# Attention units taken by TensorE two at a time instead of one at a time

## The chip, the cores and the metric

The kernel runs on one core of a Trainium2 chip. A core has TensorE (matrix products), VectorE, ScalarE and GpSimd (elementwise work), and queues that issue transfers. The engines run side by side, each through its own instruction list in order, and they meet only at semaphores: counters that one engine raises and another waits for. The profile calls the engines PE (TensorE; PEld are its weight loads), DVE (VectorE), ACT (ScalarE) and POOL (GpSimd). The metric is the device time of one execution in microseconds.

## What is computed

Two transformer blocks of two layers each, for 512 tokens of width 1024. Four of their parts are softmax attention, and only they bear on the change. The reference, cut to them:

```python
def dsa_mixer(...):                      # 12 heads, keys picked by an indexer
    s = jnp.einsum('bthd,btkd->bthk', qi, k_sel) * HEAD_DIM ** -0.5
    p = masked_softmax(s, valid[:, :, None, :]).astype(v.dtype)
    return jnp.einsum('bthk,btkd->bthd', p, v_sel)
def memory_attention(q_mem, mem_n, w_kv_mem):   # 4 heads, 256 keys, in both layers of the first block
    s = jnp.einsum('bshd,bnhd->bhsn', q, k).astype(jnp.float32) * HEAD_DIM ** -0.5
    p = jax.nn.softmax(s, axis=-1).astype(v.dtype)
    return jnp.einsum('bhsn,bnhd->bshd', p, v)
def nsa_mixer(...):                      # 12 heads, three branches, gated sum
    o = gi[..., 0:1] * o_c + gi[..., 1:2] * o_s + gi[..., 2:3] * o_w
def swa_sink_mixer(...):                 # 16 heads, this and the preceding 128 keys, a sink
    p = e / (jnp.sum(e, axis=-1, keepdims=True) + jnp.exp(sink - mx))
    o = jnp.einsum('bnkgqs,bnskd->bnqkgd', p.astype(vb.dtype), vb)
```

Everything else (projections, feed-forward parts, gated linear attention, norms) is the same before and after.

## The kernel before

**Stages.** The program is one long sequence. Most of it is 368 tiles of weights that stream in and are multiplied on TensorE (line 764). In between stand three stages of attention: stage one (names `dsa` and `mem0`), stage two (`nsa0`, `nsa1`, `mem1`) and stage three (`swa0`, `swa1`). `STREAMS` lists them and `UNITS` gives the number of units: 48, 16, 54, 54, 16, 32 and 32, in all 252.

**A unit** is one block of 128 queries of one head (in `nsa` also one of its branches) against its key tiles of 128 keys. In `dsa` the four units of a head have 1, 2, 3 and 4 key tiles. In `nsa` a head has nine units: a compressed one (one tile), and then 3, 3, 4, 4, 1, 1, 2 and 2 tiles. In `mem` every unit has 2, in `swa` a head's four units have 1, 2, 2 and 2.

**Steps of a unit g.** It passes through six steps on three engines:

- *scores* on PE (lines 955, 967): queries times keys into a score bank. There are four such banks (three for `nsa`).
- *maximum* on DVE (lines 2139, 2175): masks and finds the row maximum, written to `nmax`.
- *exponentials* on ACT (line 1583; 1579 for the compressed unit): writes the exponentials into one of two buffers, `prob[g % 2]` (the trace calls it `tmp`), and then reads out the row sum, which is the record ACTIVATION_READ_ACCUMULATOR. It waits for the maximum and for the transposes of unit g-2, which read the same buffer.
- *transposes* on PE (line 979): one per key tile, into `probT_bank[g % 2]`. They wait for the exponentials of g and for the move of g-2, which empties that bank.
- *move* on ACT (line 1598; in `dsa` and `mem` every fourth one is on DVE, line 2186): from that bank into the buffer `probT[g % 2]` (the trace calls it `sq`). It waits for the transposes of g and for the values of g-2, which read that buffer.
- *values* on PE (lines 1008, 995): transposed exponentials times values. They wait for the move of g. After them comes the output on DVE (lines 2269, 2265, 2246), which normalises.

In the trace a values product of one key tile is two MATMUL records.

**Order.** `attention_stream` (line 201) runs the same loop on each engine, with a body written for each. With u the step, ahead 4 (5 in `swa`, function `look_ahead`), the bodies are:

- PE: scores of u+4, transposes of u+2, values of u
- ACT: exponentials of u+3, move of u+2
- DVE: maximum of u+4, now and then a move of u+2, output of u

GpSimd stages the queries of the next pair of heads (lines 644 to 652) and otherwise waits in these stages. No weights are split and no product of line 764 runs in them.

Of the kernel before, what the change touches and what calls it, by code (L numbers as in the profile page):

```python
# [165 lines left out]
def attention_unit(kind, u):  # L166

    if kind.startswith("nsa"):
        hh, r = divmod(u, 9)  # L170
        return (hh, NSA_ORDER[(r - 1) // 2], 1 + (r - 1) % 2) if r else (hh, 0, 0)
    return u // 4, u % 4, 1

def compressed(kind, u):
    return kind.startswith("nsa") and u % 9 == 0
# [7 lines left out]
def look_ahead(kind):  # L184

    return 5 if kind.startswith("swa") else 4
# [7 lines left out]
def bank_of(kind, u):  # L194

    if compressed(kind, u):
        return 3
    return u % (3 if kind.startswith("nsa") else 4)
# [31 lines left out]
def key_tiles(kind, qt, branch):  # L230

    if kind.startswith("mem"):
        return list(range(N_MEM // P))
    if kind.startswith("swa"):
        return [qt - 1, qt] if qt else [0]
    return list(range(qt + 1))

def program(nc, A):
    with ExitStack() as ctx:  # L240
# [171 lines left out]
        def output_place(kind, u, g):  # L412

            if kind.startswith("swa"):
                return o_bank[g // TT % 2][:, HD * (u % TT):HD * (u % TT + 1)]
            return o_bank[g % 2][:, 0:HD]
# [144 lines left out]
        def staged(kind):  # L562

            return {"d": q_stage0, "n": q_stage1, "s": q_stage2}[kind[0]]
# [184 lines left out]
        def _(pe):  # L749
# [178 lines left out]
            def scores(kind, pair, u, i):  # L928
                hh, qt, br = attention_unit(kind, u)
                per, o, l = PER_PAIR[kind], HD * hh, int(kind[3]) if kind[3:] else 0  # L930
                g = UNIT0[kind] + pair * per + u
                out = score_bank[bank_of(kind, u)]
                if u % (per // 2) == 0:

                    pe.wait_ge(q_staged, STAGED[kind] + 2 * pair + hh + 1 + 2 * i)

                if g or not isinstance(i, int):
                    pe.wait_ge(probs_ready, g - kind.startswith(("dsa", "mem0", "swa")) + per * i)
                if compressed(kind, u):  # L940

                    if hh:
                        return
                    of_blocks = masks_b[:, 2 * P:3 * P].rearrange("p (a c) -> p a c", a=TT).unsqueeze(2).to_broadcast([P, TT, 2, 32])
                    nc.tensor.matmul(out[:, 0:2 * P], ident_b[:, :], of_blocks, start=True, stop=False)
                    for a in range(TT):
                        r = nc.tensor.matmul(out[:, 64 * a:64 * a + 64], q_pos0[:, a * P:(a + 1) * P], k_cmp[:, l, :], start=False, stop=a == TT - 1)
                    r.then_inc(scores_ready, 1)
                    return
                kts = key_tiles(kind, qt, br)  # L950
                n = len(kts) * P
                if kind.startswith("mem"):
                    if u == 0:
                        pe.wait_ge(mem_scaled, l + 1)
                    nc.tensor.matmul(out[:, 0:n], q_plain[o:o + HD, qt * P:(qt + 1) * P], k_mem[o:o + HD, l, pair, :],
                                     start=True, stop=True).then_inc(scores_ready, 1)
                    return

                q = staged(kind)[:, hh, qt * P:(qt + 1) * P]
                if kind == "dsa":  # L960
                    ks = [k[:, 0:n] for k in k_dsa]
                elif kind.startswith("swa"):
                    ks = [k[:, l, kts[0] * P:(qt + 1) * P] for k in k_swa]
                else:
                    ks = [k[:, 2 * (br - 1) + l, 0:n] for k in k_nsa]
                for part, k in enumerate(ks):
                    r = nc.tensor.matmul(out[:, 0:n], q, k, start=part == 0, stop=part == 1)  # L967

                r.then_inc(scores_ready, 2 if kind.startswith("nsa") and u == 10 else 1)

            def transposes(kind, pair, u, i):
                _, qt, br = attention_unit(kind, u)
                per = PER_PAIR[kind]
                g = UNIT0[kind] + pair * per + u
                pe.wait_ge(probs_ready, g + 3 + per * i)

                pe.wait_ge(probT_ready[g % 2], g // 2 + 1 + per // 2 * i)
                for n in range(1 if compressed(kind, u) else len(key_tiles(kind, qt, br))):
                    r = nc.tensor.transpose(probT_bank[g % 2][:, n * P:(n + 1) * P], prob[:, g % 2, n * P:(n + 1) * P], ident[:, :])  # L979
                r.then_inc(transposed, 1)  # L980

            def values(kind, pair, u, i):
                hh, qt, br = attention_unit(kind, u)
                per, l = PER_PAIR[kind], int(kind[3]) if kind[3:] else 0
                g = UNIT0[kind] + pair * per + u
                pe.wait_ge(probT_ready[g % 2], g // 2 + 2 + per // 2 * i)
                if not kind.startswith("swa"):

                    pe.wait_ge(o_done, g + 1 + per * i)
                elif u % TT == 0:  # L990

                    pe.wait_ge(o_done, g - 2 + per * i)
                if compressed(kind, u):

                    r = nc.tensor.matmul(o_bank[g % 2][:, 0:TT * HD + TT], probT[:, g % 2, 0:P], v_cmp[:, l, :], start=True, stop=True)
                    r.then_inc(pv_done, 1)
                    return
                kts = key_tiles(kind, qt, br)
                for n, kt in enumerate(kts):
                    if kind == "dsa":  # L1000
                        v = dsa_v[:, kt, :]
                    elif kind.startswith("mem"):
                        v = v_mem[:, l, kt, (2 * pair + hh) * HD:(2 * pair + hh + 1) * HD]
                    elif kind.startswith("swa"):
                        v = sv[:, kt, l * HD:(l + 1) * HD]
                    else:
                        v = v_nsa[:, kt, (br - 1) * P + l * HD:(br - 1) * P + (l + 1) * HD]
                    r = nc.tensor.matmul(output_place(kind, u, g), probT[:, g % 2, n * P:(n + 1) * P], v, start=n == 0, stop=n == len(kts) - 1)  # L1008
                r.then_inc(pv_done, 1)
# [13 lines left out]

            def pair_of_heads(per, at):

                for u in range(per):
                    later = u + look_ahead(at(u)[0])
                    if at(later):
                        scores(*at(later))
                    if at(u + 2):  # L1030
                        transposes(*at(u + 2))
                    values(*at(u))

            def concat(n, prefix, kind, units, follow, hs):

# [187 lines left out]
            def banks_free():  # L1223
                wait_evacuated(pe, "qmem0.1")

            attention_stream(pe, STREAMS[0], lambda at: attention_begin(at, banks_free), pair_of_heads)
            for l in range(DEPTH):
                if l == 1:
# [51 lines left out]
                    def banks_free():  # L1280
                        for name in ("gatesT", "qmem1.1"):
                            wait_evacuated(pe, name)

                    attention_stream(pe, STREAMS[1], lambda at: attention_begin(at, banks_free), pair_of_heads)
                concat(l, f"cat{l}", f"mem{l}", UNIT0[f"mem{l}"] + 16, f"wo{l}.0", (cat_hi, cat_lo))
                for j in range(1, KT):
# [1596 lines left out]
```

## Time and profile before

| what | value |
|---|---|
| time, median of 3 runs | 2467.14 us (2463.45 to 2471.73) |
| span of the profiled execution | 2468.0 us |
| PE busy | 2423.7 us (98%) |
| DVE busy | 936.0 us (38%) |
| ACT busy | 1079.6 us (44%) |
| POOL busy | 972.3 us (39%) |
| stage one of attention, from the trace | 144.54 to 226.22 us |
| stage two | 743.43 to 894.70 us |
| stage three | 1979.25 to 2039.27 us |

The profile is one execution; its span is 0.9 us above the median of the runs. Busy shares over the whole span mix stages with different limits, so the argument is made inside the three stages. A row of the timeline is one instruction or a run of like instructions: start, duration, engine, line, operation, output<-inputs, shapes, count, and in brackets the idle time before it with what ended that. Records of PE are pipelined: the time from the start of one to the start of the next is what it costs, and its duration, which includes the way through the array, is what somebody who waits for the result sees.

### The profile page before, as it was taken

How to read it: one execution, taken by the hardware profiler on the slowest of the kernel's cores; microseconds unless marked ns; L12 is line 12 of the kernel's file. 1: busy time of each engine (PE TensorE's matmuls, PEld its weight loads, DVE VectorE, ACT ScalarE, POOL GpSimd, SP SyncE).
4: the chain of work that ended last, by engine and by line, in shares of the span. 5: the costliest groups of instructions: out<-in, count | busy, mean ns of one | idle time of the engine just before them, and what ended most of it. 6: DMA issues, size and time to landing. Idle time of an engine off the chain costs nothing.

```text
span 2468.0 us, 36248 instructions
## 1 busy us (share of the span) xinstructions
PE 2423.7 (98%) x11990; PEld 2004.0 (81%) x11990; DVE 936.0 (38%) x2051; ACT 1079.6 (44%) x1917; POOL 972.3 (39%) x484
## 2 busy tenths in 40 slices
PE   8999999999999999999999999999999999999998
PEld 6888888888778978888887978788888797788886
DVE  7976322211477753222214243321211773311212
ACT  7565443432347754444335534432332583432321
POOL 4821444444331124444443413444443423444441
PEclk9999999999999999999999999999999999999999
DMA  4300333333420013233332312233333202233331
GB/s 154 116 30 18 90 97 101 94 102 105 128 69 10 1 35 94 93 102 93 103 102 79 103 39 81 77 95 95 100 94 94 69 18 69 86 101 95 94 94 68
DMA packets 57866, 202.75 MB, mean 82 GB/s; under 512 B 7072, under 2 KB 7968, under 8 KB 57392
## 3 DMA queue, kind: packets, MB, share of 16 engines
q1 hardware_dynamic: 54864, 196.02, 26.2%
q10 hardware_dynamic: 2912, 5.55, 0.6%
q8 instruction: 55, 0.90, 0.1%
q14 instruction: 35, 0.29, 0.0%
HBM read 199.44 MB, written 2.10 MB: 82 GB/s over the span
## 4 chain that ended last, share of the span: by engine, by line
PE 41%; issue 14%; POOL 7%; ACT 1%; DVE 1%; POOLq 0%; DVEq 0%; ACTq 0%
PE bank L764 36%; POOL w_lo L618 7%; PE bank L1008 1%; PE bank L967 1%; PE bank L979 1%; ACT h_hi L1492 1%; PE bank L1372 0%; PE bank L1353 0%; ACT gained L1495 0%; PE bank L1367 0%; PE bank L793 0%; PE bank L1055 0%; PE bank L881 0%; PE bank L770 0%; PE bank L786 0%
## 5 line engine op out<-in xcount | busy, mean ns | idle before, releaser
L618 POOL TENSOR_TENSOR w_lo<-w_raw,w_hi 128x1024 fp32r<-128x1024 f32 x368 | 883.3, 2401 | 1197.7 <-ACT w_hi L1449 1188.1
L764 PE MATMUL bank<-h_hi,w_hi 128*128 128x512 f32 x1648 | 650.5, 395 | 7.2 <-DVE tmp L2476 2.1
L764 PE MATMUL bank<-h_lo,w_hi 128*128 128x512 f32 x1648 | 642.2, 390 | 0.0
L764 PE MATMUL bank<-h_hi,w_lo 128*128 128x512 f32 x1648 | 642.2, 390 | 0.0
L1449 ACT ACTIVATE w_hi<-w_raw 128x1024 fp32r<-128x1024 f32 x368 | 386.8, 1051 | 242.7 <-PE bank L764 214.0
L764 PEld LDWEIGHTS bank<-h_hi,w_hi 128*128 128x128 f32 x1648 | 309.8, 188 | 82.3 <-issue 5.9
L764 PEld LDWEIGHTS bank<-h_hi,w_lo 128*128 128x128 f32 x1648 | 309.7, 188 | 65.2
L764 PEld LDWEIGHTS bank<-h_lo,w_hi 128*128 128x128 f32 x1648 | 309.9, 188 | 65.0 <-issue 2.2
L764 PE MATMUL bank<-mact_hi,w_hi 128*128 128x512 f32 x512 | 199.3, 389 | 1.7 <-DVEq L2342 1.7
L764 PE MATMUL bank<-mact_hi,w_lo 128*128 128x512 f32 x512 | 199.2, 389 | 0.0
L764 PE MATMUL bank<-mact_lo,w_hi 128*128 128x512 f32 x512 | 199.2, 389 | 0.0
L764 PE MATMUL bank<-act_hi,w_hi 128*128 128x512 f32 x352 | 136.9, 389 | 0.0
L764 PE MATMUL bank<-act_lo,w_hi 128*128 128x512 f32 x352 | 136.9, 389 | 0.0
L764 PE MATMUL bank<-act_hi,w_lo 128*128 128x512 f32 x352 | 136.9, 389 | 0.0
L1583 ACT ACTIVATE tmp<-bank,nmax 128x128 f32<-128x128 f32 (+2 forms) x240 | 119.1, 496 | 19.7 <-DVE nmax L2139 12.0
L2340 DVE TENSOR_TENSOR tmp<-sq,bank 128x512 f32<-128x512 f32 x64 | 44.0, 688 | 200.2 <-ACT sq L1661 200.2
L1647 ACT ACTIVATE act_hi<-tmp 128x512 f32 x44 | 27.8, 632 | 207.6 <-DVE tmp L2327 207.6
L764 PEld LDWEIGHTS bank<-mact_hi,w_hi 128*128 128x128 f32 x512 | 96.1, 188 | 21.8 <-issue 1.8
L1598 ACT ACTIVATE sq<-bank 128x128 f32<-128x128 f32 (+3 forms) x232 | 92.7, 401 | 48.1 <-PE bank L1008 44.8
L764 PEld LDWEIGHTS bank<-mact_lo,w_hi 128*128 128x128 f32 x512 | 96.1, 188 | 19.9
L764 PEld LDWEIGHTS bank<-mact_hi,w_lo 128*128 128x128 f32 x512 | 96.1, 188 | 19.8
L979 PE MATMUL bank<-ident,tmp 128*128 128x128 f32 x548 | 107.1, 284 | 3.6 <-ACT tmp L1583 1.5
(403 smaller groups left out, 3489.3 us busy)
## 6 DMA issues: line engine op xcount, KB each, us to landing
w_raw<-in_weights SPq DMA_DIRECT2D x368, 512.0 KB, 3.6
out<-x ACTq DMA_DIRECT2D x8, 256.0 KB, 2.1
x<-in_xT SPq DMA_DIRECT2D x4, 256.0 KB, 6.8
x<-in_xT ACTq DMA_DIRECT2D x4, 256.0 KB, 7.4
memx<-in_memT SPq DMA_DIRECT2D x1, 1024.0 KB, 9.8
cmp_w1k<-in_cmp_w ACTq DMA_DIRECT2D x1, 1024.0 KB, 5.6
cmp_w1v<-in_cmp_w ACTq DMA_DIRECT2D x1, 1024.0 KB, 7.5
rope_c<-in_rope_c SPq DMA_DIRECT2D x1, 256.0 KB, 8.4
```

The source lines that it names most:

```text
L618: nc.gpsimd.tensor_tensor(w_lo[:, t % RING, :], w_raw[:, t % RAW, :], w_hi[:, t % RING, :].bitcast(F32), ALU.subtract).then_inc(lo_ready, 1)
L764: r = nc.tensor.matmul(out, a, b, start=first and n == 0, stop=last and n == 2)
L967: r = nc.tensor.matmul(out[:, 0:n], q, k, start=part == 0, stop=part == 1)
L979: r = nc.tensor.transpose(probT_bank[g % 2][:, n * P:(n + 1) * P], prob[:, g % 2, n * P:(n + 1) * P], ident[:, :])
L1008: r = nc.tensor.matmul(output_place(kind, u, g), probT[:, g % 2, n * P:(n + 1) * P], v, start=n == 0, stop=n == len(kts) - 1)
L1449: nc.scalar.activation(w_hi[:, t % RING, :], w_raw[:, t % RAW, :], ACT.Copy).then_inc(hi_ready, 1)
L1492: nc.scalar.activation(h_hi[:, k, :], x_bank(k) if k < BY_PE else x[:, k, :], ACT.Identity, scale=col(name, k)).then_inc(gain_rounded, 1)
L1583: nc.scalar.activation(prob[:, g % 2, 0:n], score_bank[bank_of(kind, u)][:, 0:n], ACT.Exp, bias=nmax[:, s4:s4 + 1], scale=1.0 if kind.star ...
L1598: nc.scalar.activation(probT[:, g % 2, 0:n], probT_bank[g % 2][:, 0:n], ACT.Copy).then_inc(probT_ready[g % 2], 1)
L1647: nc.scalar.activation(act_hi[:, bass.ds(2 * i + f, 1), :].rearrange("p a n -> p (a n)"), tmp[:, f, :], ACT.Copy).then_inc(act_rounded, 1)
L2340: nc.vector.tensor_tensor(tmp[:, f % 2, :], sq[:, f % 2, :], bank[b % 2][:, :], ALU.mult).then_inc(act_made, 1)
```

## The change

Only the loop body of TensorE is written anew. It takes two steps at once: the scores of both, then the transposes of both, then the values of both. No instruction is added or removed, and the bodies of the other engines, the buffers and all the semaphore counts stay as they are.

```diff
             def pair_of_heads(per, at):
 
-                for u in range(per):
-                    later = u + look_ahead(at(u)[0])
-                    if at(later):
-                        scores(*at(later))
-                    if at(u + 2):
-                        transposes(*at(u + 2))
-                    values(*at(u))
+                for u in range(0, per, 2):
+                    for n in (u, u + 1):
+                        later = n + look_ahead(at(n)[0])
+                        if at(later):
+                            scores(*at(later))
+                    for n in (u, u + 1):
+                        if at(n + 2):
+                            transposes(*at(n + 2))
+                    for n in (u, u + 1):
+                        values(*at(n))
```

In stage one, on PE, two steps of `dsa` stood before as follows (scores are the rows with k_dsa, transposes those with ident, values those with dsa_v):

```order
L967 MATMUL bank<-k_dsa_hi,q_stage 128x128
L967 MATMUL bank<-k_dsa_lo,q_stage 128x128
L979 MATMUL bank<-ident,tmp 128x128 x3
L1008 MATMUL bank<-dsa_v,sq 128x64
L967 MATMUL bank<-k_dsa_hi,q_stage 128x256
L967 MATMUL bank<-k_dsa_lo,q_stage 128x256
L979 MATMUL bank<-ident,tmp 128x128 x4
L1008 MATMUL bank<-dsa_v,sq 128x64 x2
```

The same two steps now, in the same engine's list:

```order
L967 MATMUL bank<-k_dsa_hi,q_stage 128x128
L967 MATMUL bank<-k_dsa_lo,q_stage 128x128
L967 MATMUL bank<-k_dsa_hi,q_stage 128x256
L967 MATMUL bank<-k_dsa_lo,q_stage 128x256
L979 MATMUL bank<-ident,tmp 128x128 x7
L1008 MATMUL bank<-dsa_v,sq 128x64 x3
```

The one value product that stood between the transposes of three and of four tiles has moved behind all seven of them, and the second scores have moved ahead of the first transposes.

In stage two, on PE, where a head of `nsa` begins (v_cmp is the values product of the compressed unit), before:

```order
L967 MATMUL bank<-k_nsa_hi,q_stage 128x512
L967 MATMUL bank<-k_nsa_lo,q_stage 128x512
L979 MATMUL bank<-ident,tmp 128x128 x3
L995 MATMUL bank<-v_cmp,sq 128x260
L967 MATMUL bank<-k_nsa_hi,q_stage 128x128
L967 MATMUL bank<-k_nsa_lo,q_stage 128x128
L979 MATMUL bank<-ident,tmp 128x128 x4
L1008 MATMUL bank<-v_nsa,sq 128x64 x3
```

And now:

```order
L967 MATMUL bank<-k_nsa_hi,q_stage 128x512
L967 MATMUL bank<-k_nsa_lo,q_stage 128x512
L967 MATMUL bank<-k_nsa_hi,q_stage 128x128
L967 MATMUL bank<-k_nsa_lo,q_stage 128x128
L979 MATMUL bank<-ident,tmp 128x128 x7
L995 MATMUL bank<-v_cmp,sq 128x260
L1008 MATMUL bank<-v_nsa,sq 128x64 x3
```

Here too the values of the first unit (v_cmp) now stand behind the transposes of the unit after next but one, with its four tiles.

## Rows read from the trace of the kernel before

**Rows 1.** The page, busy time, share of the span and instructions of each engine

```profile
PE 2423.7 (98%) x11990; PEld 2004.0 (81%) x11990; DVE 936.0 (38%) x2051; ACT 1079.6 (44%) x1917; POOL 972.3 (39%) x484
```

**Rows 2.** Windows (stretch, length; busy PE, PEld, DVE, ACT, POOL; clock, DMA): dsa, mem0, nsa, swa

```profile
146.97:199.84 52.87, 52.29 (x419) 48.64 (x418) 42.08 (x187) 40.37 (x125) 7.72 (x12) 1.00 0.00 0
...
206.17:221.43 15.26, 15.26 (x90) 10.88 (x89) 9.62 (x37) 8.01 (x30) 1.47 (x2) 1.00 0.00 1
...
747.11:869.60 122.49, 121.54 (x971) 112.24 (x968) 97.30 (x432) 95.11 (x304) 14.54 (x17) 1.00 0.00 1
...
1992.31:2031.52 39.21, 39.21 (x351) 39.04 (x350) 31.87 (x146) 37.33 (x157) 9.63 (x24) 1.00 0.00 1
```

**Rows 3.** The timeline of all engines in dsa

```profile
163.09 0.56 PE L1008 MATMUL bank<-dsa_v,sq 128*128 128x64 f32 x4
...
163.74 0.60 ACT L1598 ACTIVATE sq<-bank 128x512 f32<-128x512 f32 x1 [0.21 <-PE bank L1008]
...
163.89 0.27 PE L979 MATMUL bank<-ident,tmp 128*128 128x128 f32 x1
164.00 0.78 PE L1008 MATMUL bank<-dsa_v,sq 128*128 128x64 f32 x6
...
164.24 0.47 ACT L1583 ACTIVATE tmp<-bank,nmax 128x256 f32<-128x256 f32 x1
...
164.59 0.48 PE L967 MATMUL bank<-k_dsa_hi,q_stage 128*128 128x512 f32 x1
...
164.90 0.39 PE L967 MATMUL bank<-k_dsa_lo,q_stage 128*128 128x512 f32 x1
...
165.13 0.38 PE L979 MATMUL bank<-ident,tmp 128*128 128x128 f32 x2
165.18 0.28 DVE L2269 TENSOR_SCALAR o_tok<-bank,rinv 128x64 f32 x1 [0.15 <-DVE rinv L2252]
165.35 1.00 PE L1008 MATMUL bank<-dsa_v,sq 128*128 128x64 f32 x8
165.48 0.70 DVE L2139 CUSTOM_DVE_ANT_0 bank<-bank,dsa_mask 128x512 f32<-128x512 f32 x1
...
166.09 0.14 DVE L2139 DVE_READ_ACCUMULATOR2_ANT nmax<- 128x1 f32 x1
...
166.27 0.69 ACT L1583 ACTIVATE tmp<-bank,nmax 128x512 f32<-128x512 f32 x1 [0.55 <-DVE nmax L2139]
...
168.45 0.20 ACT L1583 ACTIVATION_READ_ACCUMULATOR tmp<-bank,nmax 128x1 f32 x1
...
168.77 0.33 PE L979 MATMUL bank<-ident,tmp 128*128 128x128 f32 x1
...
168.93 0.82 PE L1008 MATMUL bank<-dsa_v,sq 128*128 128x64 f32 x6
```

**Rows 4.** Groups by shape on ACT in dsa: count, busy, mean ns, idle before

```profile
L1583 ACT ACTIVATE tmp<-bank,nmax 128x512 f32<-128x512 f32 x12 | 8.2, 687 | 5.8 <-DVE nmax L2139 5.8
...
L1598 ACT ACTIVATE sq<-bank 128x512 f32<-128x512 f32 x11 | 6.5, 594 | 1.3 <-PE bank L1008 1.1
...
L1583 ACT ACTIVATE tmp<-bank,nmax 128x128 f32<-128x128 f32 x11 | 4.0, 367 | 2.8 <-DVE nmax L2139 2.2
L1598 ACT ACTIVATE sq<-bank 128x128 f32<-128x128 f32 x12 | 3.3, 276 | 1.4 <-PE bank L1008 0.9
```

**Rows 5.** The timeline of PE in nsa, the values of a compressed unit

```profile
863.98 0.60 PE L995 MATMUL bank<-v_cmp,sq 128*128 128x260 f32 x2
```

**Rows 6.** The timeline of PE where stage one begins, scores in a row

```profile
145.49 0.40 PE L967 MATMUL bank<-k_dsa_hi,q_stage 128*128 128x512 f32 x1
145.72 0.40 PE L967 MATMUL bank<-k_dsa_lo,q_stage 128*128 128x512 f32 x1
```

**Rows 7.** Windows where stage three begins, columns as in rows 2

```profile
1979.25:1984.48 5.23, 3.59 (x24) 2.64 (x23) 4.16 (x17) 3.46 (x13) 2.61 (x3) 1.00 0.32 100
1984.48:1991.49 7.01, 7.01 (x37) 7.01 (x36) 4.79 (x16) 5.35 (x19) 0.90 (x3) 0.51 0.00 1
```

## The prediction, made before the changed kernel was run

> **What bounds the kernel now.** I read the page first: PE is busy for 98% of the span [rows 1]. The change touches only the attention stages, so the second view is the table of windows for their steady parts. In `dsa` (44 steps) PE is busy 52.29 of 52.87 us, ACT 40.37 and DVE 42.08; in `nsa` (104 steps) 121.54 of 122.49, against 95.11 and 97.30; in `mem0` (11 steps) 15.26 of 15.26 against 8.01; in `swa` (48 steps) 39.21 of 39.21, against 37.33 on ACT [rows 2]. A step thus takes 1.20, 1.18, 1.39 and 0.82 us. PE sets it everywhere, but only in `mem` with much room: the other two engines work for about four fifths of each step, and in `swa` ACT for 95%. The third view, the timeline, shows how they fit. ACT starts a move 0.09 us after the values product that frees its buffer has ended (163.09 + 0.56 = 163.65, the move at 163.74), and PE starts transposes 0.12 us after the exponentials' sum is read (168.65, then 168.77) [rows 3]. Those hand-overs lie beside other work now, because each engine has one whole step of slack against the other.
>
> **What the change adds and removes.** It removes no instruction. On PE alone it can save the switches between kinds of work. A pair of score products of four tiles costs 0.31 + 0.23 us behind a values product (164.59, 164.90, 165.13) [rows 3], and 0.23 for the first of the two when scores stand in a row (145.49, 145.72) [rows 6]. That is 0.08 us a pair of units, and one switch each from transposes to values and from values to scores goes too, for which I allow 0.05 together. So PE alone would save about 0.13 x 126 pairs = 16 us.
>
> **What it does to the order.** Call a the first unit of a pair. PE now does scores a+4, a+5; transposes a+2, a+3; values a, a+1. ACT still does move a+2, exponentials a+4, move a+3, exponentials a+5, move a+4. Follow the buffers. Move a+2 needs the values of a (same `probT`). The transposes of a+5 need the exponentials of a+5. The values of a+2 now stand behind the transposes of a+5 on PE, where they stood behind those of a+4. And move a+4, the very next item on ACT after exponentials a+5, needs the values of a+2. This is a closed ring, once per two units:
>
> values a end, 0.09, move a+2, exponentials a+4, move a+3, exponentials a+5, 0.12, transposes a+5, values a+2 end.
>
> Before, the ring went through the transposes of a+4, so move a+3 and exponentials a+5 ran on ACT while PE did transposes and values. Now all of ACT's work for two units and the round trip through PE stand one behind the other. Queued behind the waiting transposes on PE are the values of two units; behind the waiting move on ACT is everything ACT has; and the outputs on DVE follow the values.
>
> **Prices of the links.** Exponentials of one tile take 0.37 us, of four 0.69, so 0.47 and 0.58 between; a move takes 0.28 to 0.59 [rows 4]. What follows a move starts 0.10 us before its recorded end (163.74 to 164.24 for 0.60), and the read-out of a sum adds 0.10 to exponentials that somebody waits for [rows 3]. Transposes cost 0.11 us a tile (163.89 to 164.00; 165.13 to 165.35) and 0.05 more after a wait (168.77 to 168.93 for one). Values take 0.56, 0.78 and 1.00 us for two, three and four tiles, so 0.34 for one [rows 3], and 0.60 for the compressed unit [rows 5].
>
> **dsa.** With a the unit of one tile: 0.09 + move of three tiles 0.39 + exponentials of one 0.37 + move of four 0.50 + exponentials of two 0.47 + 0.10 + 0.12 + transposes of two 0.27 + values of three 0.78 = 3.09 us. With a the unit of three tiles, DVE is later than ACT, since its maximum of a+5 stands behind the output of a, and the move of a+3 is its own: 0.09 + output 0.30 + maximum of four tiles 0.75 + 0.04 (165.18, 165.48, 166.23, 166.27 [rows 3]) + exponentials 0.79 + 0.12 + transposes of four 0.49 + values of one 0.34 = 2.92. A head takes 6.01 instead of 4.81 us, and 44 steps are 11 heads: **+13 us**. From below, if the round trip hides 0.2 us of each ring, +9; from above, if one hand-over more of 0.2 us falls into each, +18.
>
> **nsa.** Two heads are 18 units and nine rings. The moves sum to 5.8 us (16 of them at 0.18 to 0.50, two compressed at 0.18), the exponentials to 8.4 and, as an estimate for the two compressed ones, 0.4, the nine read-outs to 0.9 and the nine double hand-overs to 1.9. The transposes of a+5 have 21 tiles in the nine rings, so 2.3 + 9 x 0.05 = 2.8, and the values of a+2 sum to 0.78 + 1.00 + 0.34 + 0.56 + 0.78 + 1.00 + 0.34 + 0.56 + 0.60 = 6.0. That is 26.2. In three or four rings DVE's maximum, or the eight products of the compressed scores on PE, comes later than ACT; I add 0.4 and take 26.6 against 18 x 1.18 = 21.2. With 104 steps, 5.8 such groups: **+31 us**, with +26 and +37 as ends.
>
> **swa.** PE is five ahead here and ACT four, so exponentials a+6 fill the round trip, and the ring is 0.09 + move a+2 + exponentials a+5 + move a+3 + 0.12 + transposes a+5 + values a+2: 0.09 + 0.27 + 0.47 + 0.37 + 0.12 + 0.27 + 0.56 = 2.15 us, and with a move and values of one tile 1.83, to which the exponential of the sink adds some 0.1. A head takes 4.07 instead of 3.27 us. With 59 steps that is +11.8, less a little for the five that stand at the lower clock already: **+11 us**, with +7 and +15 as ends.
>
> **mem.** PE takes 2.78 us for two units. The ring is 0.09 + 0.28 + 0.47 + 0.28 + 0.47 + 0.10 + 0.12 + 0.27 + 0.56 = 2.64, so PE still sets the time: **0**, with -3 (the switches) and +3 as ends.
>
> The PE-only saving is not added anywhere, since PE waits in each of these rings; if `mem` shows it, it is in the -3. GpSimd's staging and the weights' queue gain time and stay hidden: POOL is busy 7.72 of 52.87 us and waits for scores [rows 2].
>
> **Sum.** 13 + 31 + 11 + 0 = 55 us. The profiled execution would go from 2468.0 to 2523, and the median of the runs, 0.9 us lower, from 2467 to 2522. The ends of the terms together give +39 to +73.
>
> **Rivals.**
>
> *The clock falls (slower still).* Where stage three begins, PE was busy 3.59 of 5.23 us and then ran 7.01 us at a granted clock of 0.51, which is mostly the lower level of 1.2 GHz against 2.4; that stretch holds five steps, 1.40 us each against 0.82 [rows 7], [rows 2]. After the change PE will be without work for about a fifth of three stages, some 300 us. For it: PE busy shares there come near those 69%. Against it: the idle is in slices of half a microsecond between runs of products, and the present stages hold the full clock. A step at the low clock costs 1.40 us where I expect 1.0 in `swa`. If a fifth of about 280 us ran so, +20 us more, so 2542; if half did, +50, so 2572. The Trainium skill, "TensorE: Matmul & The Clock Gate", section "A second HAM failure mode: psum-queue depth-cycling", says that frequent short idles between groups of matmuls make the clock swing between its levels; by that rule this rival is the likelier one. The granted clock of 1.00 through the four stretches of rows 2 neither shows nor excludes it, since PE is never short of work there.
>
> *PE's own saving decides (faster).* If ACT and DVE kept up, the switches would be all that counts: 2467 - 16 = 2451. It decides where the ring of two units is shorter than PE's work for two: below 2.4 us in `dsa`, where I find 2.9 to 3.1. For it: ACT has a fifth of its time free in `dsa` and `nsa`, and the buffers are not fewer. Against it: the ring is made of waits that the code fixes, and ACT's free fifth is no help to it, since the ring puts that time where ACT has nothing it may start. The Trainium skill, same page, section "Loop structure matters more than you think", recommends dense runs of PE work with the other engines behind; by it the answer would be this rival's.
>
> *The slack swallows it (no change).* If half a step of slack were left that I do not see, each ring would fall back under PE's time, and saving and waits would cancel: 2467, at most 7 to either side.
>
> *A milder loss.* If in `nsa` the moves, short for units of one tile, let ACT run ahead, so that only every second ring closes: 13/2 + 31/2 + 11/2 = 28, so 2495.
>
> **Chances.** My ring 0.74, the clock 0.13, the milder loss 0.07, no change 0.02, PE's saving 0.04. About 0.3%, or 7 us, is what a measurement of this kernel can tell from no change. So faster 0.04, same 0.02, slower 0.94. The range takes the ends of the sum, +39 to +73, is widened below to +33 for part of the milder case, and reaches above to +93 for the clock in a fourth of the stages: 2500 to 2560.
>
> **What would show it.** In the profile of the changed kernel, windows in `dsa`, `nsa` and `swa` should show PE busy near 80% and ACT near what it had in microseconds, with step times of 1.50, 1.48 and 1.02 us, and `mem` unchanged near 1.39. The waits should show transposes of odd units waiting for exponentials, and ACT's moves of even units waiting for values for 0.8 to 1.5 us each. The ring is wrong if PE stays over 95% busy there, if the moves wait for something else, or if the added time lies outside the stages. A granted clock below 1 in the steady parts would show the first rival.

## The result, and the profile after

The changed kernel takes 2519.65 us (median; 2518.39 to 2523.78), against 2468.76 us for the kernel before in the same comparison. The ratio is 1.0212, with a 95% interval of 1.0198 to 1.0226. The profiled execution went from a span of 2468.0 us to 2518.0.

The page of the changed kernel has as first line, busy time, share and instructions, where [rows 1] stood:

```profile
PE 2441.4 (97%) x11990; PEld 2001.7 (79%) x11990; DVE 930.1 (37%) x2051; ACT 1070.8 (43%) x1917; POOL 972.2 (39%) x484
```

That line hides the change. PE's busy time is even larger by 18 us. A record of PE reaches past the start of the next one (transposes of one tile last 0.27 us where the next start is 0.11 on, [rows 3]), and ahead of a wait nothing covers that tail: in `dsa` 22 waits go with 3.3 us more busy time. The instructions of ACT and DVE are the same in number, and their busy times within 1%. The time shows in windows. These are the five stretches of attention in the changed kernel, in the columns of [rows 2]: `dsa` from its first step, `mem0` to the end of its stage, `nsa`, `mem1`, and the whole of `swa`:

```profile
148.74:213.34 64.60, 55.63 (x421) 48.54 (x419) 40.14 (x186) 37.65 (x124) 8.12 (x12) 1.00 0.00 0
213.34:238.56 25.22, 23.95 (x156) 19.24 (x155) 15.15 (x67) 13.44 (x50) 2.52 (x2) 1.00 0.01 2
758.05:912.18 154.13, 136.99 (x970) 114.05 (x968) 96.37 (x432) 90.49 (x304) 14.97 (x17) 1.00 0.00 1
912.18:937.22 25.04, 23.66 (x145) 17.52 (x144) 14.26 (x63) 13.00 (x50) 2.52 (x2) 1.00 0.01 1
2021.69:2090.51 68.82, 59.59 (x468) 52.47 (x466) 45.46 (x198) 52.88 (x211) 13.66 (x31) 1.00 0.03 9
```

The first and the third answer to the lines of `dsa` and `nsa` in [rows 2]. For the other three, the kernel before has, from scores of the same units to the same place:

```profile
199.84:226.22 26.38, 25.78 (x156) 18.90 (x155) 16.02 (x65) 14.17 (x48) 2.88 (x3) 1.00 0.01 2
...
869.60:894.75 25.15, 24.55 (x145) 17.67 (x144) 15.92 (x61) 13.83 (x49) 2.99 (x3) 1.00 0.00 1
1979.25:2039.27 60.02, 57.18 (x468) 55.57 (x466) 45.97 (x198) 52.31 (x211) 13.54 (x31) 0.94 0.03 10
```

So `dsa` went from 52.87 to 64.60 us (+11.7), `mem0` by -1.2, `nsa` from 122.49 to 154.13 (+31.6), `mem1` by -0.1 and `swa` from 60.02 to 68.82 (+8.8). That sums to 50.8 us where the spans differ by 50.0: the whole loss lies inside the attention stages. PE's weight loads (the second of the busy figures) fall from 92% of the stretch to 75% in `dsa` and to 74% in `nsa`, and ACT from 76% and 78% to 58% and 59%. Nobody is busier; everybody waits.

For whom is in the waits of the changed kernel (its lines from 1030 on are three higher than before: 1601 is the move, 1586 the exponentials, 2142 the maximum, 2272 the output). Columns: who waited for whom, us in total, times, longest. First `dsa`, 22 pairs:

```profile
ACT sq L1601 <- PE bank L1008: 23.7, 22, 1.2
DVE o_tok L2272 <- PE bank L1008: 19.0, 22, 1.4
PEld bank L979 <- ACT tmp L1586: 14.4, 22, 0.8
```

Then `nsa`, 52 pairs:

```profile
ACT sq L1601 <- PE bank L1008: 55.9, 51, 1.4
...
PEld bank L967 <- ACT tmp L1586: 19.7, 36, 0.8
...
PEld bank L979 <- ACT tmp L1586: 13.7, 30, 0.7
...
ACT sq L1601 <- PE bank L995: 7.2, 6, 1.2
```

Once in each pair ACT's move waits 1.1 us for values, and in `dsa` once in each pair PE waits for exponentials before transposes. Each waits for the other in turn. In `nsa` PE stands more often before scores (line 967, 36 times) than before transposes (30 times). By the code, with three score banks the second scores of the next pair, a+7, need the bank that exponentials a+4 read, and these follow the move that waits for the values of a. It is the same ring, met one item earlier on PE: at 800.03 us scores have waited 0.64 us for exponentials, and at 801.08 the transposes behind them wait 0.15 more.

The ring's two turns of one head, from the timeline of the changed kernel in `dsa`:

```profile
174.30 0.49 ACT L1601 ACTIVATE sq<-bank 128x384 f32<-128x384 f32 x1 [0.92 <-PE bank L1008]
...
174.68 0.36 ACT L1586 ACTIVATE tmp<-bank,nmax 128x128 f32<-128x128 f32 x1
...
175.03 0.60 ACT L1601 ACTIVATE sq<-bank 128x512 f32<-128x512 f32 x1
...
175.50 0.48 ACT L1586 ACTIVATE tmp<-bank,nmax 128x256 f32<-128x256 f32 x1
...
175.86 0.22 ACT L1586 ACTIVATION_READ_ACCUMULATOR tmp<-bank,nmax 128x1 f32 x1
176.13 0.44 PE L979 MATMUL bank<-ident,tmp 128*128 128x128 f32 x2 [0.45 <-ACT tmp L1586]
...
176.41 1.67 PE L1008 MATMUL bank<-dsa_v,sq 128*128 128x64 f32 x14
177.28 0.28 ACT L1601 ACTIVATE sq<-bank 128x128 f32<-128x128 f32 x1 [1.20 <-PE bank L1008]
...
177.65 0.70 DVE L2142 CUSTOM_DVE_ANT_0 bank<-bank,dsa_mask 128x512 f32<-128x512 f32 x1
...
178.44 0.69 ACT L1586 ACTIVATE tmp<-bank,nmax 128x512 f32<-128x512 f32 x1 [0.32 <-DVE nmax L2142]
...
179.28 0.66 PE L979 MATMUL bank<-ident,tmp 128*128 128x128 f32 x4 [0.35 <-ACT tmp L1586]
...
179.77 0.78 PE L1008 MATMUL bank<-dsa_v,sq 128*128 128x64 f32 x6
180.20 0.49 ACT L1601 ACTIVATE sq<-bank 128x384 f32<-128x384 f32 x1 [0.98 <-PE bank L1008]
```

Read it from the top: move, exponentials, move, exponentials on ACT without a gap; 0.05 us after the sum is read, PE's transposes; then the values (the record of 14 holds those of two units, three and four tiles); and 1.20 us after ACT had stopped, the next move. From move to move the first turn takes 2.98 us and the second, in which ACT also waits 0.32 us for DVE's maximum, 2.92.

### The profile page after: what moved, and what is told of

Read it like the earlier page. It is cut to its first block, busy times and chain, and to the rows that moved or that the text cites. A ratio compares the mean times of both kernels' runs of the same rounds, so it can differ in the third digit from the quotient of the medians.

```text
span 2518.0 us, 36242 instructions
## 1 busy us (share of the span) xinstructions
PE 2441.4 (97%) x11990; PEld 2001.7 (79%) x11990; DVE 930.1 (37%) x2051; ACT 1070.8 (43%) x1917; POOL 972.2 (39%) x484
## 4 chain that ended last, share of the span: by engine, by line
PE 39%; issue 15%; POOL 7%; ACT 2%; DVE 1%; POOLq 0%; ACTq 0%; DVEq 0%
PE bank L764 35%; POOL w_lo L618 6%; PE bank L1008 1%; PE bank L979 1%; PE bank L1375 0%; ACT h_hi L1495 0%; ACT tmp L1586 0%; ACT sq L1601 0%; PE bank L1356 0%; PE bank L1370 0%; PE bank L793 0%; ACT gained L1498 0%; PE bank L798 0%; PE bank L881 0%; PE bank L770 0%
## 5 line engine op out<-in xcount | busy, mean ns | idle before, releaser
L979 PE MATMUL bank<-ident,tmp 128*128 128x128 f32 x548 | 101.6, 284 | 25.5 <-ACT tmp L1586 16.8
```

## The experiments

All are made on the order of one part at a time, or on one tie at a time. The table gives, from the trace of each, the time from the first scores of a kind to the first scores of the next kind, or to the end of the stage (first turning of the outputs), and the median time with its ratio to the kernel before, run beside it. In `swa` the kernel before had a stretch at the low clock [rows 7] that no other profile in the table has; the others are to be held against the 57.3 us of scores_paired and not against its 60.0.

| kernel | dsa | mem0 | nsa | mem1 | swa | time, us | ratio (95% interval) |
|---|---|---|---|---|---|---|---|
| before | 55.3 | 26.4 | 125.3 | 25.2 | 60.0 | 2466 to 2469 | |
| the changed kernel | 67.0 | 25.2 | 156.9 | 25.0 | 68.8 | 2519.65 | 1.0212 (1.0198 to 1.0226) |
| scores_paired | 55.2 | 23.8 | 131.1 | 22.9 | 57.3 | 2467.25 | 1.000 (0.9991 to 1.001) |
| transposes_paired | 69.8 | 28.1 | 161.2 | 26.9 | 69.0 | 2530.56 | 1.0259 (1.0242 to 1.0276) |
| after_four | 63.7 | 24.5 | 148.0 | 23.5 | 62.9 | 2499.51 | 1.0134 (1.0117 to 1.0151) |
| after_ahead | 57.4 | 25.9 | 157.0 | 25.2 | 68.8 | 2512.97 | 1.0187 (1.0170 to 1.0204) |
| after_five | 57.4 | 25.9 | 145.8 | 27.0 | 68.5 | 2499.95 | 1.0135 (1.0118 to 1.0152) |
| after_four_five | 55.1 | 25.2 | 135.6 | 25.8 | 62.7 | 2481.88 | 1.0063 (1.0046 to 1.0080) |
| after_all | 53.1 | 24.9 | 125.2 | 24.3 | 59.3 | 2463.60 | 0.9991 (0.9982 to 1.0001) |
| before_five | 52.9 | 27.4 | 122.1 | 26.1 | 57.3 | 2462.08 | 0.9978 (0.9968 to 0.9987) |
| before_four_five | 52.6 | 27.2 | 120.7 | 25.9 | 57.0 | 2459.88 | 0.9972 (0.9962 to 0.9981) |
| mix_two | 51.2 | 24.5 | 122.1 | 24.8 | 57.0 | 2455.83 | 0.9951 (0.9936 to 0.9966) |
| best_mix | 50.6 | 24.3 | 120.7 | 24.6 | 56.7 | 2452.96 | 0.9946 (0.9933 to 0.9960) |

**Scores alone in pairs** (scores_paired), the edit against the kernel before:

```diff
-                for u in range(per):
-                    later = u + look_ahead(at(u)[0])
-                    if at(later):
-                        scores(*at(later))
-                    if at(u + 2):
-                        transposes(*at(u + 2))
-                    values(*at(u))
+                for u in range(0, per, 2):
+                    for n in (u, u + 1):
+                        later = n + look_ahead(at(n)[0])
+                        if at(later):
+                            scores(*at(later))
+                    for n in (u, u + 1):
+                        if at(n + 2):
+                            transposes(*at(n + 2))
+                        values(*at(n))
```

> Only the scores are taken two at a time: scores a+4, a+5, then transposes a+2, values a, transposes a+3, values a+1. The ring theory: values of a+2 again stand right behind the transposes of a+4, so no ring closes; what is left is the switch saved, about 0.08 us a pair in 100 pairs, so some 8 us under the kernel before: 2460 (2455 to 2468), and at least 50 us under the changed kernel. The rival, that having two scores in a row holds up the others (banks, a later start of the transposes): half or more of the 51 us loss stays, over 2490.

Measured: 2467.25 us, inside the range but at its upper end, and the same as before. The loss is not in the pairs of scores. But the 8 us of saved switches are not there either. In `swa`, where PE has no idle time, one pair reads:

```profile
2012.69 0.36 PE L967 MATMUL bank<-k_swa_hi,q_stage 128*128 128x256 f32 x1
2012.89 0.28 PE L967 MATMUL bank<-k_swa_lo,q_stage 128*128 128x256 f32 x1
2013.01 0.28 PE L967 MATMUL bank<-k_swa_hi,q_stage 128*128 128x256 f32 x1
2013.13 0.28 PE L967 MATMUL bank<-k_swa_lo,q_stage 128*128 128x256 f32 x1
2013.25 0.38 PE L979 MATMUL bank<-ident,tmp 128*128 128x128 f32 x2
2013.47 0.33 PE L1008 MATMUL bank<-sv,sq 128*128 128x64 f32 x2
2013.66 0.41 PE L979 MATMUL bank<-ident,tmp 128*128 128x128 f32 x2
2013.91 0.56 PE L1008 MATMUL bank<-sv,sq 128*128 128x64 f32 x4
2014.27 0.36 PE L967 MATMUL bank<-k_swa_hi,q_stage 128*128 128x256 f32 x1
```

The second product of the second scores starts 0.12 us after the first, where it takes 0.20 behind values: that is the 0.08 I had counted. But now transposes stand behind values, and there the same price is paid: a one-tile values product takes 0.19 us to the next start and a two-tile run of transposes 0.25, against 0.14 and 0.22 in the other order. PE still leaves values twice a pair, once for scores and once for transposes, and the pair takes 1.58 us (2012.69 to 2014.27) where the same pair takes 1.59 in the order one at a time; the last section has both. In `nsa` the stretch is even 5.8 us longer. It has three score banks, and scores wait there for exponentials; the waits of that stretch have

```profile
PEld bank L967 <- ACT tmp L1585: 9.6, 23, 0.5
```

where the kernel before has no such wait among its largest. That these waits are the 5.8 us was not tested by itself; ACT's moves wait longer there too. In the two `mem` stretches pairs of scores do save, 2.6 and 2.3 us.

**Transposes alone in pairs** (transposes_paired), the edit against the changed kernel:

```diff
-                    for n in (u, u + 1):
-                        later = n + look_ahead(at(n)[0])
-                        if at(later):
-                            scores(*at(later))
+                    if at(u + look_ahead(at(u)[0])):
+                        scores(*at(u + look_ahead(at(u)[0])))
                     for n in (u, u + 1):
                         if at(n + 2):
                             transposes(*at(n + 2))
-                    for n in (u, u + 1):
-                        values(*at(n))
+                    values(*at(u))
+                    if at(u + 1 + look_ahead(at(u + 1)[0])):
+                        scores(*at(u + 1 + look_ahead(at(u + 1)[0])))
+                    values(*at(u + 1))
```

> Only the transposes are taken two at a time: scores a+4, transposes a+2, a+3, values a, scores a+5, values a+1. The ring theory: values of a+2 stand behind the transposes of a+5 as in the changed kernel, so the whole loss is there without pairs of scores or values: 2520 (2510 to 2532). The rival, that the loss comes from scores or values in pairs: under 2490.

Measured: 2530.56 us, in the range, and 11 us over the changed kernel. So the loss needs neither pairs of scores nor adjacent values; two runs of transposes ahead of the values are enough. That it is worse still fits the second scores standing between the values of a and those of a+1, for which move a+3 waits; it was not tested by itself.

**More buffers between move and values** (after_four). The transposed exponentials get four buffers (three in `nsa` and `mem1`), in space of the activations that is unused during attention:

```diff
+            k = u % 3 if kind.startswith("nsa") else (u + 3) % 4 if kind == "mem1" else g % 4
+            return sq[:, k, part] if k < 2 else more_T[:, k - 2, part]
...
-                act.wait_ge(pv_done, g + 1 + per * i)
-                nc.scalar.activation(probT[:, g % 2, 0:n], probT_bank[g % 2][:, 0:n], ACT.Copy).then_inc(probT_ready[g % 2], 1)
+                moves_free(act, kind, g, per, i)
+                nc.scalar.activation(probT_of(kind, u, g, slice(0, n)), probT_bank[g % 2][:, 0:n], ACT.Copy).then_inc(probT_ready[g % 2], 1)
```

`moves_free` waits for the values of four (three) units back.

> The changed kernel with four buffers for the transposed exponentials (three in nsa and mem1), so that a move waits for the values of four (three) units back and not of two. Ring theory: the link from values to the next move is gone. In swa nothing else ties the engines, so its whole loss goes (about -10 us). In dsa and nsa a second ring stays, through DVE: values a, output a, maximum a+5, exponentials a+5, transposes a+5, values a+2: 0.09 + 0.30 + 0.6 + 0.04 + 0.65 + 0.12 + 0.33 + 0.67 = 2.8 us a pair, against 2.9 to 3.0 now and 2.4 before; so -5 us in dsa and -5 to -10 in nsa. In all 2498 (2488 to 2508). If the buffers had nothing to do with it: 2520 with no stage changed. If they were the only tie: about 2460.

Measured: 2499.51 us, 20 us off the changed kernel's time with PE's order untouched. `dsa` gave back 3.3 us where I had put 5, and `nsa` 8.9. The second ring, through DVE, is in the waits of `dsa` in this kernel (line 1600 is the exponentials, 2286 the output, 1022 the values):

```profile
ACT tmp L1600 <- DVE nmax L2156: 18.8, 29, 1.2
DVE o_tok L2286 <- PE bank L1022: 15.7, 22, 1.2
```

ACT no longer waits 23.7 us for values. It waits for maxima, and once in each pair DVE's output, which stands before the maximum, waits for values. `swa` gave back 5.9 us, not all: something else ties it too. The timeline of `swa` in this kernel shows it (the transposes are line 993):

```profile
2030.67 0.37 ACT L1600 ACTIVATE tmp<-bank,nmax 128x128 f32<-128x128 f32 x1 [0.65 <-PE bank L993]
...
2034.38 0.37 ACT L1600 ACTIVATE tmp<-bank,nmax 128x128 f32<-128x128 f32 x1 [0.66 <-PE bank L993]
```

Exponentials wait for the transposes of two units back, which read the same one of two buffers.

**Five ahead** (after_ahead in `dsa` and `mem0`, after_five everywhere):

```diff
-    return 5 if kind.startswith("swa") else 4
+    return 5 if kind.startswith("swa") or kind in ("dsa", "mem0") else 4
```

> The changed kernel with dsa and mem0 five scores ahead as swa is (exponentials four ahead), buffers as they were. Ring theory: exponentials a+6 now fill the round trip, and DVE's maximum a+5 comes before output a. Rings of a dsa head: 0.09 + 0.39 + 0.47 + 0.60 + 0.12 + 0.27 + 0.78 = 2.72 and about 2.4 (PE's own), so 5.1 us a head instead of 5.9: -9 us, in dsa alone: 2511 (2507 to 2515). The rival, that PE's own order costs the time: 2520 unchanged.

Measured: 2512.97 us; `dsa` went from 67.0 to 57.4 us (-9.6), `mem0` grew by 0.7. That is a test inside one kernel: `nsa` and `swa`, which were not edited, stayed at 157.0 and 68.8.

> The changed kernel with five scores ahead in every kind, so in nsa and mem1 too (which have three score banks); buffers as they were. Ring theory: in nsa exponentials a+6 fill the round trip and the ring is 0.09 + 0.33 + 0.53 + 0.43 + 0.12 + 0.31 + 0.66 = 2.5 us a pair on average against 3.0 in the changed kernel: -25 us in nsa beside the -9 in dsa: 2488 (2480 to 2500). The rival, that nsa is held by its three banks of scores: no gain over five ahead in dsa alone, 2513.

Measured: 2499.95 us, at the upper end. `nsa` gave back 11 us, not 25. So five ahead is not enough there.

**Both together** (after_four_five).

> The changed kernel with both: four (three) buffers and five ahead everywhere. Ring theory: the ring over ACT and the one over DVE are both open, so PE's own work sets the time again with the order two at a time in full: no more than before, 2455 to 2470. If taking two units at a time costs PE itself something: 2480 or more remains.

Measured: 2481.88 us, 12 us over the range. Here my theory of two rings fell short: `dsa` was at the kernel before's time (55.1 us), but `nsa` was 10 us and `swa` some 5 over what PE needs. The next run asks whether that is the tie that after_four had shown, or PE's order itself.

**More buffers for the exponentials too** (after_all), against after_four_five:

```diff
-                act.wait_ge(transposed, g + 1 + per * i)
+                deep = 3 if kind.startswith("nsa") or kind == "mem1" else 4
+                free = g + 3 - deep
+                act.wait_ge(transposed, max(free, 1) if isinstance(i, int) and not i else free + per * i)
```

> The changed kernel, five ahead everywhere, four (three) buffers for the transposed exponentials and now also four (three) for the exponentials themselves, so that exponentials wait for the transposes of four (three) units back. What is left of the loss with five ahead and the first four buffers is 13 us, +10 in nsa and +5 in swa. If it is the tie from transposes to the exponentials of two units on (a third ring): swa falls to the kernel before's and nsa by half or more, in all 2470 (2464 to 2475). If it is the score banks, or PE's order in itself: 2479 to 2484 as before this edit.

Measured: 2463.60 us, ratio 0.9991, just below the range. With the changed order of PE in full, and only waits taken out of the other engines' way by buffers and by looking ahead, the kernel is as fast as the kernel before. `nsa` is at 125.2 us with three score banks as ever, so the banks alone did not hold it. Windows of `dsa`, `nsa` and `swa` in this kernel:

```profile
145.92:198.98 53.06, 51.98 (x415) 48.67 (x413) 40.52 (x188) 39.56 (x125) 7.39 (x11) 1.00 0.00 0
739.52:864.68 125.16, 123.76 (x964) 114.39 (x963) 92.59 (x433) 94.01 (x305) 13.72 (x16) 1.00 0.02 5
1971.84:2031.18 59.34, 56.02 (x468) 52.44 (x466) 44.70 (x198) 51.47 (x211) 14.01 (x31) 1.00 0.04 10
```

PE is at 98%, 99% and 94% of them, and its weight loads, the better measure of the two, at 92%, 91% and 88%.

**The same edits in the order one at a time** (before_five, before_four_five).

> The kernel before with five ahead everywhere. PE waits for transposes there for some 10 to 15 us in dsa and nsa, most of it behind late maxima; those go: 2459 (2454 to 2467). If PE's idle there is its own: 2467.

> The kernel before with five ahead everywhere and four (three) buffers for the transposed exponentials. No ring is near PE's time there, so the buffers add nothing to five ahead: within 3 us of it, 2459. If the buffers matter in the order one at a time too: 2450 or less.

Measured: 2462.08 and 2459.88 us. Five ahead is worth 0.2%, in `dsa` (-2.4 us) and `nsa` (-3.1); the buffers, worth 20 us in the changed kernel, give about 2 here, with overlapping intervals. These two are also the fair measure of after_all, which has the same look-ahead and one more set of buffers: at 0.9991 (0.9982 to 1.0001) it does not reach the 0.9972 (0.9962 to 0.9981) of before_four_five. The two intervals only just miss each other. In the traces `nsa` is at 125.2 us against 120.7 and `swa` at 59.3 against 57.0, and the `mem` stretches give back 3.9 of these 7 us. So even with the slack bought, taking all of the work two at a time is no faster than one at a time. What still costs it time in `nsa` and `swa` is left open.

**A mix** (best_mix, mix_two): one at a time, five ahead, scores in pairs outside `nsa`, with four buffers and with two.

```diff
-                    later = u + look_ahead(at(u)[0])
-                    if at(later):
-                        scores(*at(later))
+                    pairs = not at(0)[0].startswith("nsa")
+                    for n in (() if pairs and u % 2 else (u, u + 1) if pairs else (u,)):
+                        later = n + look_ahead(at(n)[0])
+                        if at(later):
+                            scores(*at(later))
```

> The order one at a time, five ahead and four buffers, and scores alone in pairs in dsa, mem and swa, not in nsa with its three score banks. Ring theory: pairs of scores close no ring, and in mem they saved about 2 us a stage when scores alone were paired: 2455 (2451 to 2460), so 4 to 5 us under five ahead with four buffers. If pairs of scores are worth nothing: 2460.

> The same with the two buffers of the kernel before. With no ring near PE's time in the order one at a time, the buffers are worth 2 us at most: 2457 (2453 to 2462). If they carry the gain: 2462 or more.

Measured: 2452.96 us (ratio 0.9946) and 2455.83 us (0.9951). Both beat the kernel before by half a per cent, and the one with two buffers needs no more room than it. About half of that is five ahead; the pairs of scores add the rest, as mix_two (0.9951) against before_five (0.9978) shows. They save in `mem` (2.9 and 1.3 us) and in `dsa` (1.7), and 0.3 in `swa`.

## Why the prediction was right

It said 2522 us for the median and 2523 for the profiled execution; these were 2519.65 and 2518.0. It added 55 us, and the windows show 50.8. Part of how near the median came is luck: the kernel before took 2468.76 us in this comparison and not the 2467 that the sum started from. By its steps:

- **The closed ring.** Shown. It is in the timeline of `dsa` above as it was written down, and it opens and closes with its links: transposes in pairs close it, scores in pairs don't, more buffers behind the move open part of it, and filling the round trip by looking ahead opens it in the one kind where that is done.
- **dsa, +13.** It was +11.7. The two turns take 2.98 and 2.92 us where the sum had 3.09 and 2.92. The first is shorter because PE starts 0.05 us after the read-out instead of 0.12, and each of ACT's items starts 0.01 to 0.03 sooner behind the one before. That DVE's maximum would be the later one in the second turn was right.
- **nsa, +31.** It was +31.6, and a step takes 1.48 us, as said. The sum named only the waits before transposes; the 36 waits of scores were not in it. They lie inside the same turn and, as the sum came out, did not lengthen it; that they add nothing was not tested by itself.
- **swa, +11.** It was +8.8, but the kernel before had spent five steps of this stage at the low clock [rows 7] and the changed one none (granted clock 1.00 in its window). Those steps cost 1.40 us in place of 0.82, so 2.9 us came back from there. Against the stretch of scores_paired, which had no low clock either, 57.3 us, the ring cost 11.5.
- **mem, 0.** It was -1.2 and -0.1. In the middle of `mem0` a pair takes PE 2.78 us before, 2.48 to 2.55 in the changed kernel (scores start at 226.99, 229.54 and 232.02) and 2.44 in scores_paired. So in `mem0` PE saved 0.2 to 0.3 us a pair, more than the 0.13 of the sum, and the ring came out shorter than the 2.64 it was put at. In `mem1` a pair takes 2.66 us (scores start at 922.44, 925.10 and 927.77). In `mem0` part of the saving is given away at the ends of the stage, where `dsa` units are still in the pairs and where the last transposes wait 0.54 us for exponentials.
- **The saving on PE**, 0.13 us a pair, was wrong outside `mem`. A `dsa` head takes PE 4.58 us one at a time (before_four_five, 170.67 to 175.25) and 4.58 in the changed order where it does not wait (after_all, 163.12 to 167.70), and a `swa` pair 1.59 and 1.58. What scores in a row save, values in a row cost; the last section shows it. Scores alone in pairs bring a `dsa` head to 4.49 (best_mix, 171.75 to 176.24). The saving was in no term of the sum, since PE waits anyway, so it did no harm. As the price of the rival that forecast a gain, 16 us was far too high.
- **The clock.** The rival with the second largest chance did not come: the granted clock is 1.00 in all five stretches, although PE's weight loads are busy for only three quarters of 288 us of them. The Trainium skill, "TensorE: Matmul & The Clock Gate", section "A second HAM failure mode: psum-queue depth-cycling", tells of a kernel in which frequent short idles made the clock swing. This trace does not agree for idle slices of the size it has: 0.35 and 0.45 us in the turns above, 0.64 in `nsa`.
- **The signs to look for.** ACT's moves waited 1.08 us each in `dsa` and 1.10 in `nsa`, inside the 0.8 to 1.5 named; in `swa`, where exponentials fill the trip, less. But PE's busy share was 86%, 89% and 87%, not near 80%: the tail of a record ahead of a wait counts as busy. PEld, at 75%, 74% and 76%, is the better column for this.
- **What was not seen.** A third tie, from transposes to the exponentials of two units on, lay just under the first two. It changes nothing in this sum, but it is why after_four_five kept 13 us.

## What to carry to other kernels

Where engines hand work round through pairs of buffers, write down the ring: each item, and who must finish before it may start, until you are back at the first. Grouping an engine's work by kind puts one more item between a producer and its consumer on that engine, and if the ring's sum then exceeds the busiest engine's time for the same units, every turn costs the difference, however idle the other engines look. The slack has to be bought first, with one more buffer or one step more of look-ahead at each tie; and the grouping is worth trying on the one kind of work that closes no ring. Here that was the scores, outside the stage that has only three banks for them; all of the work in groups, with the slack bought, was no faster than the old order with the same slack.

## What the runs showed of the hardware

A matmul's price depends on what stands before it. In `mem0` of the kernel before, one unit's scores (two records, contraction over 64 rows) take 0.62 us to the next start (206.17 to 206.79):

```profile
206.17 0.70 PE L955 MATMUL bank<-k_mem,diag 64*128 64x256 f32 x2
206.79 0.44 PE L979 MATMUL bank<-ident,tmp 128*128 128x128 f32 x2
```

Two units' scores in a row, in scores_paired, take 1.06 (206.67 to 207.73), so 0.53 each:

```profile
206.67 1.13 PE L955 MATMUL bank<-k_mem,diag 64*128 64x256 f32 x4
207.73 0.44 PE L979 MATMUL bank<-ident,tmp 128*128 128x128 f32 x2
```

For values the price is seen only together with what follows. In `swa` of the kernel before, a pair of units one at a time takes 1.59 us (1999.90 to 2001.49):

```profile
1999.90 0.36 PE L967 MATMUL bank<-k_swa_hi,q_stage 128*128 128x256 f32 x1
...
2000.44 0.33 PE L1008 MATMUL bank<-sv,sq 128*128 128x64 f32 x2
2000.58 0.36 PE L967 MATMUL bank<-k_swa_hi,q_stage 128*128 128x256 f32 x1
...
2001.12 0.56 PE L1008 MATMUL bank<-sv,sq 128*128 128x64 f32 x4
2001.49 0.36 PE L967 MATMUL bank<-k_swa_hi,q_stage 128*128 128x256 f32 x1
```

The same pair in the changed order, in after_all where PE does not wait, takes 1.58 (1990.07 to 1991.65):

```profile
1990.07 0.36 PE L985 MATMUL bank<-k_swa_hi,q_stage 128*128 128x256 f32 x1
...
1990.62 0.60 PE L997 MATMUL bank<-ident,more_P 128*128 128x128 f32 x4
1991.06 0.78 PE L1026 MATMUL bank<-sv,sq 128*128 128x64 f32 x6
1991.65 0.36 PE L985 MATMUL bank<-k_swa_hi,q_stage 128*128 128x256 f32 x1
```

The scores have fallen from 0.64 to 0.55 us, the transposes stand at 0.44 in both, and the values have risen from 0.14 + 0.37 to 0.59. A values product of one tile thus shows 0.14 us to the next start before scores, 0.19 before transposes and about 0.22 before other values, and scores behind values show 0.08 more than scores behind scores. In `swa` the 0.08 us that I had read as the price of a switch is what is left of the values, whatever follows them.
